# Dense products of a decoder step: tokens split at 304 in place of 260, and two passes of the last 216 tokens in one matmul of 432 columns

## What is computed

```python
# layer 0: x += W_out [ dilated attention || causal pooling ] ( W_in RMSNorm(x) )
# layer 1: x += gated DeltaNet ( RMSNorm(x) )
# both:    x += SwiGLU( RMSNorm(x) ),  then a final RMSNorm
def _swiglu(h, wg, wu, wd):
    return (jax.nn.silu(h @ wg) * (h @ wu)) @ wd      # hidden width 2816
```

## Time and profile before

| | before |
| --- | --- |
| time, median (lowest to highest) | 1709.58 us (1704.66 to 1716.78) |
| span of the profiled execution, first to last instruction | 1703.2 us |
| granted TensorE clock, mean | 0.916 |
| TensorE busy | 1613.1 us, 95% |
| weight loads busy | 1518.8 us, 89% |
| VectorE busy | 850.8 us, 50% |
| ScalarE busy | 515.6 us, 30% |
| GpSimd busy | 219.7 us, 13% |

### The profile page before, as it was taken

The page is one execution under the profiler, slowest core; times in us unless marked ns, Lnnn a source line. Parts: engine busy times, 40 slices in busy tenths (PEclk is TensorE's granted clock), DMA queues, the critical chain, the costliest instruction groups (busy, mean ns, idle before and its releaser), DMA issues.

```text
span 1703.2 us, 30528 instructions
## 1 busy us (share of the span) xinstructions
PE 1613.1 (95%) x11944; PEld 1518.8 (89%) x11944; DVE 850.8 (50%) x1268; ACT 515.6 (30%) x783; POOL 219.7 (13%) x183
## 2 busy tenths in 40 slices
PE   6999999999999999979999999998879999999998
PEld 5995588999999999978998889887769999999997
DVE  5445512544344334666667666765435443443343
ACT  4122112332122222433343344333224221221234
POOL 5410000200000000213212321231112000000002
PEclk8995555999999999989999999997579999999999
DMA  5345200464355322312122122110022332332322
GB/s 168 87 125 142 56 1 13 124 215 161 116 168 186 98 86 84 90 50 51 40 63 60 42 64 62 51 51 25 27 64 86 90 96 87 91 94 88 94 77 87
DMA packets 229888, 147.25 MB, mean 86 GB/s; under 512 B 5172, under 2 KB 223817, under 8 KB 229412
## 3 DMA queue, kind: packets, MB, share of 16 engines
q1 hardware_dynamic: 227984, 140.63, 28.0%
q0 software_dynamic: 1520, 5.65, 1.1%
q10 hardware_dynamic: 332, 0.24, 0.0%
HBM read 137.31 MB, written 26.36 MB: 96 GB/s over the span
## 4 chain that ended last, share of the span: by engine, by line
PE 84%; DVE 8%; issue 4%; ACT 2%; POOL 1%; DMA 1%; DVEq 0%; SPq 0%; ACTq 0%; POOLq 0%
PE acc L625 53%; PE acc L843 7%; PE aux L934 6%; PE aux L764 2%; PE aux L742 2%; PE aux L916 2%; PE aux L926 2%; DVE y L1704 1%; PE aux L1067 1%; DVE w_lo L1435 1%; PE aux L1040 1%; PE acc L798 1%; PE acc L887 1%; PE acc L797 1%; PE acc L777 1%
## 5 line engine op out<-in xcount | busy, mean ns | idle before, releaser
L1435 DVE TENSOR_TENSOR w_lo<-w_raw,w_hi 128x1024 fp32r<-128x1024 f32 x200 | 265.4, 1327 | 123.9 <-ACT w_hi L1136 117.9
L1136 ACT ACTIVATE w_hi<-w_raw 128x1024 fp32r<-128x1024 f32 x200 | 209.9, 1050 | 231.2 <-PE acc L625 212.2
L625 PE MATMUL acc<-h_hi,w_hi 128*128 128x260 f32 x1664 | 220.2, 284 | 4.8 <-ACT h_hi L1148 4.0
L625 PE MATMUL acc<-h_lo,w_hi 128*128 128x260 f32 x1664 | 218.6, 284 | 0.7 <-DVE h_lo L1442 0.7
L625 PE MATMUL acc<-h_hi,w_lo 128*128 128x260 f32 x1664 | 217.5, 283 | 0.0
L625 PEld LDWEIGHTS acc<-h_hi,w_hi 128*128 128x128 f32 x1664 | 207.6, 189 | 6.8 <-ACT h_hi L1148 5.3
L625 PEld LDWEIGHTS acc<-h_lo,w_hi 128*128 128x128 f32 x1664 | 208.0, 190 | 1.5 <-DVE h_lo L1442 1.5
L625 PEld LDWEIGHTS acc<-h_hi,w_lo 128*128 128x128 f32 x1664 | 207.7, 190 | 0.0
L1928 POOL TENSOR_TENSOR ssum<-ssum,sq 128x520 f32<-128x520 f32 x40 | 56.2, 1404 | 977.4 <-issue 859.9
L625 PE MATMUL acc<-g_hi,w_hi 128*128 128x260 f32 x928 | 125.3, 286 | 8.9 <-ACT g_hi L1175 5.1
L625 PEld LDWEIGHTS acc<-g_hi,w_hi 128*128 128x128 f32 x928 | 117.4, 191 | 11.6 <-ACT g_hi L1175 6.3
(11 more groups left out here) (307 smaller groups left out, 2138.6 us busy)
## 6 DMA issues: line engine op xcount, KB each, us to landing
w_raw<-in_w_ffn_gate SPq DMA_DIRECT2D x44, 512.0 KB, 3.8
w_raw<-in_w_ffn_up SPq DMA_DIRECT2D x44, 512.0 KB, 3.8
w_raw<-in_w_ffn_down SPq DMA_DIRECT2D x32, 512.0 KB, 4.0
w_raw<-in_w_in_c SPq DMA_DIRECT2D x32, 512.0 KB, 4.1
w_raw<-in_w_in_a SPq DMA_DIRECT2D x16, 512.0 KB, 4.0
w_raw<-in_w_ffn_down SPq DMA_DIRECT2D x16, 384.0 KB, 3.3
w_raw<-in_w_out_a SPq DMA_DIRECT2D x8, 512.0 KB, 4.0
s_in<-in_state_gdn SPq DMA_DIRECT2D x8, 512.0 KB, 4.0
```

Source lines behind the costliest of these rows:

```text
L625: last = nc.tensor.matmul(acc[:, 2 * slot + b, 0:TH], w[:, slot, k * P:(k + 1) * P], x[:, k, b * TH:(b + 1) * TH], start=part == 0 and k == 0,
L1136: nc.scalar.activation(w_hi[:, slot], w_raw[:, slot], ACT.Copy).then_inc(w_hi_made, 1)
L1435: nc.vector.tensor_tensor(w_lo[:, slot], w_raw[:, slot], w_hi[:, slot].bitcast(F32), ALU.subtract).then_inc(w_lo_made, 1)
```

## The change

The activations' hi and lo parts move into one tensor each (`h_both`, `g_both`, with the old names for its halves), so that one access pattern reads both. The tokens are split at TA = 304 (TB = 216). In a slot the first 304 tokens take the last 304 columns of the first bank, the other 216 the first 216 of the second, so the 520 columns are contiguous over the two banks. For each k-tile with w_hi there are now three matmuls: 304 columns of hi, 304 of lo, and one of 432 columns that reads the last 216 tokens of hi and of lo and writes two accumulators side by side (columns 0 to 215 and 216 to 431 of the second bank). With w_lo there are two, of 304 and 216 columns. The order is k-tile by k-tile over the first three, then k-tile by k-tile over w_lo; the wait for hi and that for lo of a tile stand together. The eviction adds the second accumulator: `add_to_stream` gets a second addition of 216 columns, `scaled` a multiplication of 216 columns into `rest` ahead and an addition of 216 behind; each waits for the operation whose result it changes, by a new semaphore `acc_taken` of VectorE to itself. The sixths and the first two w_out_c products are cut anew to the same numbers of columns, and the transposed tails lie at columns 0 to 127.

```diff
+TA = 304
+TB = T - TA
+        rest = sb("rest", TB)
-        h_hi = sb("h_hi", [KD, T], F32R)
-        h_lo = sb("h_lo", [KD, T], F32R)
+        h_both = sb("h_both", [2, KD, T], F32R)
+        h_hi, h_lo = h_both[:, 0], h_both[:, 1]
...
         def accv(slot):
-            return acc[:, 2 * slot:2 * slot + 2, 0:TH]
+            return acc[:, 2 * slot:2 * slot + 2].rearrange("p b t -> p (b t)")[:, 512 - TA:512 + TB]
+        def acc_rest(slot):
+            return acc[:, 2 * slot + 1, TB:2 * TB]
...
+            def first_part(slot, w, x, k, first):
+                bank_a, bank_b = acc[:, 2 * slot, 512 - TA:512], acc[:, 2 * slot + 1, 0:2 * TB]
+                wk = w[:, slot, k * P:(k + 1) * P]
+                nc.tensor.matmul(bank_a, wk, x[:, 0, k, 0:TA], start=first, stop=False)
+                nc.tensor.matmul(bank_a, wk, x[:, 1, k, 0:TA], start=False, stop=False)
+                nc.tensor.matmul(bank_b.rearrange("p (r t) -> p r t", r=2), wk, x[:, :, k, TA:T], start=first, stop=False)
+            def last_part(slot, x, k, last):
+                wk = w_lo[:, slot, k * P:(k + 1) * P]
+                nc.tensor.matmul(acc[:, 2 * slot, 512 - TA:512], wk, x[:, 0, k, 0:TA], start=False, stop=last)
+                return nc.tensor.matmul(acc[:, 2 * slot + 1, 0:TB], wk, x[:, 0, k, TA:T], start=False, stop=last)
+            def product(n, slot, kt, x, hi_at=None, lo_at=None):
...
-                for part, (w, x, ready) in enumerate(((w_hi, xh, hi_at), (w_hi, xl, lo_at), (w_lo, xh, None))):
-                    if part == 2:
-                        pe.wait_ge(w_lo_made, n + 1)
-                    for k in range(kt):
-                        if ready:
-                            pe.wait_ge(*ready(k))
-                        for b in range(2):
-                            last = nc.tensor.matmul(acc[:, 2 * slot + b, 0:TH], w[:, slot, k * P:(k + 1) * P],
-                                                    x[:, k, b * TH:(b + 1) * TH], start=part == 0 and k == 0,
-                                                    stop=part == 2 and k == kt - 1)
+                for k in range(kt):
+                    if hi_at:
+                        pe.wait_ge(*hi_at(k))
+                        pe.wait_ge(*lo_at(k))
+                    first_part(slot, w_hi, x, k, k == 0)
+                pe.wait_ge(w_lo_made, n + 1)
+                for k in range(kt):
+                    last = last_part(slot, x, k, k == kt - 1)
                 last.then_inc(acc_full, 1)
...
             def add_to_stream(n, m, slot):
                 dve.wait_ge(acc_full, n + 1)
-                nc.vector.tensor_tensor(halves(xT[:, m]), accv(slot), halves(xT[:, m]), ALU.add).then_inc(acc_read, 1)
+                nc.vector.tensor_tensor(xT[:, m], accv(slot), xT[:, m], ALU.add).then_inc(acc_taken, 1)
+                dve.wait_ge(acc_taken, n + 1)
+                nc.vector.tensor_tensor(xT[:, m, TA:T], acc_rest(slot), xT[:, m, TA:T], ALU.add).then_inc(acc_read, 1)
             def scaled(out, n, slot):
                 dve.wait_ge(acc_full, n + 1)
-                nc.vector.tensor_tensor(halves(out), accv(slot), halves(rstd), ALU.mult).then_inc(acc_read, 1)
+                if not isinstance(n, int) or n:
+                    dve.wait_ge(acc_read, n)
+                nc.vector.tensor_tensor(rest[:], acc_rest(slot), rstd[:, TA:T], ALU.mult)
+                nc.vector.tensor_tensor(out, accv(slot), rstd[:], ALU.mult).then_inc(acc_taken, 1)
+                dve.wait_ge(acc_taken, n + 1)
+                nc.vector.tensor_tensor(out[:, TA:T], out[:, TA:T], rest[:], ALU.add).then_inc(acc_read, 1)
```

More of the change, by code:

```diff
@@ L706, in _ @@
             for n in range(16):
-                product(N_IN_A + n, n % 2, KD, h_hi, h_lo, **(normed(0) if n == 0 else {}))
+                product(N_IN_A + n, n % 2, KD, h_both, **(normed(0) if n == 0 else {}))
                 if n == 0:
@@ L823, in _ @@
             for n in range(KD):
-                product(N_OUT_A + n, n % 2, KD, g_hi, g_lo)
+                product(N_OUT_A + n, n % 2, KD, g_both)
             ffn(1, N_FFN0, 0)
@@ L837, in product_sixth @@
                     pe.wait_ge(w_lo_made, n + 1)
-                w, x = ((w_hi, h_hi), (w_hi, h_lo), (w_lo, h_hi))[j // 2]
-                for k in range(4 * (j % 2), 4 * (j % 2) + 4):
-                    if isinstance(n, int) and n == N_IN_C and j < 4:
-                        pe.wait_ge(*normed(2)["hi_at" if j < 2 else "lo_at"](k))
-                    for b in range(2):
-                        last = nc.tensor.matmul(acc[:, 2 * slot + b, 0:TH], w[:, slot, k * P:(k + 1) * P],
-                                                x[:, k, b * TH:(b + 1) * TH], start=j == 0 and k == 0, stop=j == 5 and k == KD - 1)
+                if j < 4:
+                    for k in (2 * j, 2 * j + 1):
+                        if isinstance(n, int) and n == N_IN_C:
+                            pe.wait_ge(*normed(2)["hi_at"](k))
+                            pe.wait_ge(*normed(2)["lo_at"](k))
+                        first_part(slot, w_hi, h_both, k, k == 0)
+                else:
+                    for k in range(4 * (j - 4), 4 * (j - 4) + 4):
+                        last = last_part(slot, h_both, k, k == KD - 1)
                 if j == 5:
@@ L881, in out_third @@
                         pe.wait_ge(gb[e].sem, gb[e].all(GH - 1))
-                if part == 2 and heads[0] == 0:
+                if part == 1 and heads[0] == 0:
                     pe.wait_ge(w_lo_made, N_OUT_C + m + 1)
-                w, x = ((w_hi, g_hi), (w_hi, g_lo), (w_lo, g_hi))[part]
                 for k in heads:
-                    for b in range(2):
-                        last = nc.tensor.matmul(acc[:, 2 * m + b, 0:TH], w[:, m, k * P:(k + 1) * P], x[:, k, b * TH:(b + 1) * TH],
-                                                start=part == 0 and k == 0, stop=part == 2 and k == GH - 1)
-                return last
+                    if part == 0:
+                        first_part(m, w_hi, g_both, k, k == 0)
+                    else:
+                        last = last_part(m, g_both, k, k == GH - 1)
+                return last if part else None
             def turn(it, g_on, a_on, b_on):
@@ L1099, in _ @@
             for m in range(2):
-                for part in range(3):
-                    last = out_third(m, part, [GH - 1])
+                for part in range(2):
+                    last = out_part(m, part, [GH - 1])
                 last.then_inc(acc_full, 1)
```

32 lines of the change are left out of this document (16 added, 16 removed).

## The result

| | before | after |
| --- | --- | --- |
| time, median of four runs each (lowest to highest) | 1713.18 us (1704.66 to 1717.23) | 1742.99 us (1741.72 to 1746.21) |
| span of the profiled execution | 1703.2 us | 1739.5 us |
| granted TensorE clock, mean | 0.916 | 0.914 |

The ratio is 1.0214, with a 95% interval from 1.0176 to 1.0252: the change makes the kernel 2.1% slower. Run again beside other runs of before it gave 1.0239 (1.0198 to 1.0280). The forecast was 1728, +18 us on the span; the span grew by 36.3. The medians grew by 29.8 here and by 40.4 in the second comparison, since before ran at 1705 there.

A forecast was written before the change was run, and what follows sets the result against it. TensorE, busy 95%, was taken as the bound, mostly by dense products. 14 + 1.5 - 2 + 3 + 1.4 = +18 us gave 1721 on the profile, 1728 on the median; own range 1715 to 1742 (chance 0.42), wider range 1665 to 1760.

The forecast's parts named there:

- 1.5 + 3 + 1.4: Exposed longer evictions: first down products +1.5 us, delta-rule turns +3, z_turned and the last tile +1.4.
- Dense products, +14: All dense products: a k-tile's five matmuls take 726.4 ns, 8.8 more, over 1568 k-tiles: +14 us.
- The bound taken: Matmul price: about 2.3 ns fixed plus 0.451 ns a column, so 304 columns cost 139.4 ns and 432 cost 197.2.
- Rival 1: Dense matmuls: all 11.3 ns beyond the columns are a fixed price per matmul; +2 us, 1712; chance 0.18.
- rival 2: Dense matmuls: 119.6 ns is a floor for one matmul with its load; -45 us, rest +4, 1669; chance 0.16.
- rival 3: Narrow matmuls: under 260 columns float32r falls to the plain pace, 363 ns for 216; 2123 us; chance 0.14.
- Starts of the down products, +1.5: First down product of a part, six times: TensorE waits longer for hi and lo together; 1 to 2 us more.
- Norm, -2: First product after a norm: 7 k-tiles cover the last tile, cutting the 4.0 us wait for h_hi; -2 us.
- Evictions outside the turns, taken as 2.9: Outside delta-rule turns: steady loops covered; only first down products (+1.5) and z_turned with the last tile (+1.4) cost.
- Delta-rule turns, +3 of a range 0 to 7: Eight delta-rule turns: three of four evictions covered by VectorE's idle time, the second costs 0 to 0.85 us a turn.
- rise toward 26: Delta-rule stage: TensorE's 22.0 us wait for line 1719 was to stay under 26 us.
- Rival 4: Delta-rule stage: VectorE becomes the bound, delaying each of 8 turns by 3.4 us; +27 us, 1752; chance 0.10.

The follow-up runs named there:

- seventh run: Changed kernel with one-operation evictions everywhere except the four of each delta-rule turn, which stay long (some products lack columns): ratio 1.0071, median 1714.9 us.
- eleventh run: Changed kernel with the eight small transposes ahead of the first delta-rule turn done eight times over, nothing else: ratio 1.0144, median 1728.0 us.
- first run: Changed kernel with all evictions in one operation, the second accumulator not read, matmuls unchanged: ratio 1.0051, median 1717.1 us.

## Why the prediction was wrong, step by step

The sign was right and 1743 lies in the range, but above the forecast's own 1715 to 1742. The step that failed is the one that called the longer evictions covered: 1.5 + 3 + 1.4 = 5.9 us in the sum, 19 in the runs at equal clock. The change of the clock had no term. Each term:

- **Dense products, +14: right.** 726.2 ns a k-tile against 726.4, 13.6 us in all. The bound taken, 2.3 ns fixed and 0.451 ns a column, gives 139.4 and 197.2; 140 and 196.5 were read. Rival 1 (a fixed price, 1712) would have had 191 for 432 columns and 716 for the k-tile, rival 2 (a floor) 129 for 304 columns, rival 3 363 for 216. None is seen. The place of the narrow matmul's price was off (the pair is 151 and 99, not 139 and 111), its sum wasn't. The split at 264 shows that this price is all of the dense loss.
- **Starts of the down products, +1.5: right in kind.** g_hi's 5.1 us in the earlier trace rows became 6.0 for g_both.
- **Norm, -2: its reason was wrong.** Of h_hi's 4.0 us, 3.8 lie before 60 us, at the first norm, where no eviction is near; the sum could have gained only what lies elsewhere. I had said that "some" of it belonged there and took half. After waits 6.8 for h_both, 6.1 of it before 60 us, since hi and lo are now both wanted. That the order alone saves about 2 us at equal clock (1558.4 against 1560.8) is luck for the size.
- **Evictions outside the turns, taken as 2.9 (1.5 and 1.4): about 11 at equal clock.** Part of it is ScalarE's list behind the longer eviction: the conversion to w_hi queues behind the norm's work in a last down part, 3.5 us of waits in the first feed-forward, where before has 0.5. The prediction named what is behind the eviction "on VectorE's queue" and called the steady loops covered. With 6 k-tiles a product isn't enough cover. Of the 11 us, 10.1 are seen at full clock in the two feed-forwards (6.1 and 4.0); the table of stages hides part of them, since the order saves 1.5 and 0.7 us there. Most of the 6.1 are waits; the 4.0 aren't traced.
- **Delta-rule turns, +3 of a range 0 to 7: about 8 at equal clock, and the clock on top.** VectorE's idle behind each eviction had looked like cover, but TensorE waits for other results behind them too. The range took one exposed eviction of 0.85 us a turn (a working that comes to 0.91: two operations of 0.38 and a wait of 0.15); the turn pays 1.2, more of it for the three evictions called covered than for z_k. Waits in after, over the whole kernel:

```profile
PE aux L956 <- DVE ip L1748: 16.0, 17, 2.3
PE acc L934 <- DVE zc L1481: 12.3, 10, 5.9
...
PE aux L938 <- ACT egb L1342: 5.2, 6, 3.2
```

The wait for `ip` didn't rise toward 26, it fell from 22.0 to 16.0, and a wait for the eviction of zc stands beside it, five times 0.9 us in the five turns, where before has it once (3.3 us), ahead of them. In the first five turns of the window 17.1 us at half clock became 41.0, which at 0.42 us each is 10 of the 17.5 us that they grew by; of the rest 5.9 are the evictions and 1.4 the 20 products (20 x 8 x 8.7 ns). Over the whole stage half clock went from 116 to 130 us, since the stretch ahead of the turns had less of it: some 6 of the 15.7 us that are left there. The other 9 or so are what eight turns of 1.2 us make.
- **Rival 4 (VectorE binds, all 3.4 us a turn, 1752)** is near in time and wrong in its mechanism. At equal clock a turn pays 1.2 us, not 3.4; after's turns are 61.2 and 61.8 where before has 58.0, so 3.2 to 3.8, only because the clock comes on top. The seventh and eleventh run show the same turns at 58.0.

Shown is that the same turns, with the same instructions, have run in 290.1 and 307.3 us over five, in step with the time at half clock, and that a change ahead of them moves it. Which feature of a turn brings the clock down is not shown, and neither is why after ran at 1740.2 to 1746.5 in all eight executions while the seventh run's kernel spreads over 25 us. Of the 28 us that the first run gave back, 19 are work at equal clock and the other 9 the clock, 0.916 against 0.912.

## What to carry to other kernels

When an eviction is lengthened, follow every engine that reads its result, and each one's list behind that read: one stall came from a conversion that has nothing to do with the eviction and only stood behind it. Idle time of the evicting engine is not cover; here 200 evictions, 0.5 to 0.9 us longer each, cost 19 us while VectorE was busy 50%. Before joining matmuls to save one, look at the narrowest that remains; one fewer was worth nothing here, and one of 216 columns cost 8.7 ns a k-tile. In a loop whose clock changes between its two levels, compare lengths at equal clock (length times granted clock) first, and hold no small edit of it good or bad by its time alone.

## What the runs showed of the hardware

- A float32r matmul with 128 x 128 weights goes from start to start in 119.6 ns for 260 columns, 140 for 304, 196.5 for 432: a line of 2.3 ns and 0.451 ns a column. The Trainium skill, "TensorE: Matmul & The Clock Gate", section "Back-to-back issue gap", would have 129 and 182.5 for the last two (N / 2.4 + 2.5, its isolated gap of one matmul); the trace doesn't agree for float32r.
- Pairs of 304 and 216 columns, each with its own weight load, take 249 ns, pairs of 264 and 256, with the same sum of columns, 241. The extra time shows at the matmul after the narrow one (151 ns in place of 140 for 304 columns). An uncovered load of 112 ns would do this; the load alone was never varied.
- A 216-column float32 operation of VectorE takes 383 ns in the feed-forwards and, at the median, 385 on `zc` in the delta-rule stage, where single ones are longer, up to 2114. What lengthens those wasn't tried.
- The same 1937 matmuls and their neighbours on the other engines ran at a mean clock of 0.93 in one kernel and 1.00 in another, and took 307.3 and 290.1 us: 0.42 us for each us at half clock.
